# The last group of a convolution feed-forward layer written out, its down units run together, and the last stores cut smaller

## The chip, the cores and the metric

One core of a Trainium2 chip runs the kernel. The metric is device time in microseconds (us), the median of several runs. The kernel before took 2371.83 us (three runs, 2370.70 to 2373.25).

## What is computed

One decoder layer for 512 prompt tokens and 8 sample tokens, 2048 channels wide, everything in f32:

```python
h = RMSNorm(x); z = h @ w_in                      # mixers A, B, C from slices of z
x += concat(A, B, C) @ w_out
z = RMSNorm(x) @ w_up                             # 2048 -> 2 x 5632
zc = conv_b + sum(zp[:, j:j+T] * conv_w[j] for j in range(3))   # causal, depthwise, width 3
g, a = split(zc);  x += (silu(g) * a) @ w_down    # 5632 -> 2048
# outputs, among others: x (y_prompt, y_sample) and the last two rows of z before the convolution
# (ffn_conv_prompt; for the samples the new row, ffn_conv_sample)
```

The change touches only the feed-forward part and the outputs named in the last comment.

## The kernel before, in words

Tokens lie along the free dimension: `xT` holds 16 channel tiles of 128 partitions by 520 tokens (512 + 8). A matmul has a 128x128 weight block as stationary operand and half of the tokens, 260, as moving operand. For accuracy each f32 weight block is split into a rounded part and a rest, `whi` and `wlo`, and so are the activations, and three products are added: hi*hi, hi*lo, lo*hi. The work is cut into **units** of 1 MB of weights, each of four **quarters**; a quarter is 3 products x 4 blocks x 2 halves = 24 matmuls. For each quarter ACT copies raw weights to `whi` (`q_hi`, L812), POOL subtracts to get `wlo` (L1633), and TensorE (PE) runs the matmuls. `whi` and `wlo` are rings of four quarters, so ACT may convert a quarter when PE has done the quarter four before it (semaphore `w_used`); `raw` holds two units, filled by SyncE (SP) with `load_pair` (L1659) when POOL has split the unit two before.

The 44 tiles of the hidden layer go in 11 **groups** of four (`GC` = 4, `NG` = 11). A group has 8 **up units** (for each of its four tiles one for g and one for a, `up_mm`, matmuls at L415) and 4 **down units** (`down_mm`, L709), in which each quarter makes one of the 16 output tiles. For tile j the vector engine (DVE) reads the two up results (`read`, L1525, and the last 10 columns into `ztail`, L1528), ACT and DVE do the convolution (`conv`, L1538 and L1540), ACT the SiLU, DVE the gate `gm` (L1553), ACT `g_hi` (L1092), DVE `g_lo` (L1558). DVE also adds each down quarter into `xT` (semaphore `d_add`); quarters alternate between two PSUM bank pairs, so down quarter n waits for the addition of n-2.

The order is written out by hand for each engine, with semaphores between. Group 0 does its 8 ups. In the loop over groups 1 to 10, the order of one pass is: two ups of this group, the four down units of the **previous** group, the other six ups. So a group's gates are ready long before its downs, except in the last: behind the loop stand only the downs of group 10, which need the gate of the last tile (`g_lo` >= `NG*GC`), made from the last up unit.

Behind the loop PE also does three kinds of transposes. `turn_tail` (L769) turns four `ztail` tiles of 10 columns at a time, 22 times in all: six before the last downs, one behind each of the last down quarters but the first, and one at the very end; ACT reads each result to `trow` (L1124). `turn_y(dt)` (L778) turns output tile dt to token-major, one quarter behind the additions, and DVE reads it to `ytok` (L1147). At the end, when all tails are read, 16 transposes (L799) turn the sample tokens, and one ACT copy reads them (L1143). SP stores `y_prompt` in four pieces of four tiles (1 MB); before the fourth it waits for all tails and stores `trow` as two transfers, one of 2 partitions and one of 8, each partition 11264 floats long. The sample store is last, and SP waits for every store before it ends (L1751).

Of the kernel before, what the change touches and what calls it, by code (L numbers as in the profile page):

```python
# [21 lines left out]
F32 = mybir.dt.float32  # L22
# [5 lines left out]
P = 128  # L28
D = 2048
# [29 lines left out]
U_GRP = 2 * GC  # L59
U_ALL = U_FFN + NG * (U_GRP + GC)  # L60


# [18 lines left out]
def hybrid_layer(nc, io):  # L81
# [217 lines left out]
    par_rows = Region(fA.at, 2 * GC * P * 4).take("par_rows", [20, 2, GC * P])  # L299
    ytok = fA.take("ytok", [P, NB, D])  # L300
    fZ = r_z.again()
    trow = fZ.take("trow", [S + 2, F2])
    ytok8 = fZ.take("ytok8", [S, D])

    sems = {}
# [95 lines left out]
    def _(pe):  # L401
# [297 lines left out]

        def down_mm(q0, d0):  # L700

            for k in range(4):
                pe.wait_ge(w_lo, q0 + (k + 1))
                pe.wait_ge(s("d_add"), d0 + (k + 1))
                b = 4 + 2 * (k % 2)
                for kind, (w, x) in enumerate(((whi, g_hi), (whi, g_lo), (wlo, g_hi))):
# [55 lines left out]

        def turn_tail(r):

            b = 2 + r % 2
            if r >= 2:
                pe.wait_ge(s("t_read"), r - 1)
            for c in range(4):
                t = nc.tensor.transpose(ps[0:S + 2, b, c * P:(c + 1) * P], ztail[:, 4 * r + c, :], ident[:])  # L769
            t.then_inc(s("t_turn"), 1)  # L770

        def turn_y(dt):

            pe.wait_ge(s("d_add"), (NG - 1) * 16 + dt + 3)
# [6 lines left out]
        pe.wait_ge(z_free, U_FFN + 8 * NG + 2)  # L781
        tails = iter(range(FC // 2))
        for _ in range(6):
            turn_tail(next(tails))
        pe.wait_ge(s("g_lo"), NG * GC)
        for m in range(GC):
            for k in down_mm(4 * (U_ALL - GC + m), (NG - 1) * 16 + 4 * m):
                if 4 * m + k >= 1:
                    turn_y(4 * m + k - 1)
                    turn_tail(next(tails))  # L790
        turn_y(15)
        turn_tail(next(tails))
        assert next(tails, None) is None
        pe.wait_ge(s("t_read"), FC // 2)
        for q in range(4):
            if q == 0:
                pe.wait_ge(s("d_add"), NG * 16 + 2)
            for c in range(4):
                t = nc.tensor.transpose(ps[0:S, 4 + q, c * P:(c + 1) * P], xT[:, 4 * q + c, T:N], ident[:])  # L799
        t.then_inc(s("y8_turn"), 1)  # L800


    @block.scalar
    def _(act):
# [285 lines left out]
        def gated_hi(n, j):  # L1090
            act.wait_ge(s("f_m"), n + 1)
            nc.scalar.activation(g_hi[:, j, :], gm[:], ACT.Copy).then_inc(s("g_hi"), 1)  # L1092

        def ffn_group_act(q1, pair0, n0, grp, with_down):


            nonlocal n_group
            n_group = grp
            units = GC * 3 if with_down else U_GRP
            due = {} if with_down else {(1, 3): [(norm_root, 0)]}  # L1100
            for j in range(GC):
# [6 lines left out]
                due.setdefault(hi_at, []).append((gated_hi, j))  # L1108
            for u in range(1, units + 1):
                for k in range(4):  # L1110
                    q_hi(q1 + (4 * (u - 1) + k), k, u % 2, pair0 + 16 * (u // 2))
                    for step, j in due.get((u, k), []):
# [4 lines left out]
        n_group = 0  # L1117
        ffn_group_act(4 * U_FFN + 4, 8 * U_FFN + 16, 0, 0, False)
        with act.Fori(1, NG) as i:
            ffn_group_act(i * 48 + 4 * (U_FFN + U_GRP - 12 + 1), i * 96 + 8 * (U_FFN + U_GRP - 12 + 2), i * GC, i, True)  # L1120

        def read_tail(r):
            act.wait_ge(s("t_turn"), r + 1)
            nc.scalar.activation(trow[:, 512 * r:512 * r + 512], ps[0:S + 2, 2 + r % 2, :], ACT.Copy).then_inc(s("t_read"), 1)  # L1124

        r = 0
        for u in range(U_ALL - GC, U_ALL):
            for k in range(4):
                if u > U_ALL - GC:
                    q_hi(4 * u + k, k, u % 2, 16 * (u // 2 + 1))  # L1130
                    reads = 1
                else:
                    reads = 2
                for _ in range(reads):
                    if r < 6 or u > U_ALL - GC:
                        if r < FC // 2:
                            read_tail(r)
                            r += 1
        while r < FC // 2:
            read_tail(r)  # L1140
            r += 1
        act.wait_ge(s("y8_turn"), 1)
        nc.scalar.activation(ytok8[:], ps[0:S, 4:8, :].rearrange("p a n -> p (a n)"), ACT.Copy).then_inc(s("y8_read"), 1)  # L1143

# [7 lines left out]
    def _(dve):  # L1152
# [358 lines left out]

        def ffn_group_dve(u0, n0, d0, base, tail, with_down):

# [42 lines left out]
            def lo(n, j):  # L1556
                dve.wait_ge(s("g_hi"), n + 1)
                tt(g_lo[:, j, :], gm[:], g_hi[:, j, :].bitcast(F32), sub).then_inc(s("g_lo"), 1)  # L1558

            def down(m, k):  # L1560
                e = 4 * m + k
                dve.wait_ge(w_used, u0 * 4 + (4 * (2 + m) + k + 5))
                x2 = halves(xT[:, e, :])
                tt(x2, pair(4 + 2 * (k % 2)), x2, add).then_inc(s("d_add"), 1)  # L1564

            for j in range(GC):
                g = 2 * j + (GC if with_down and j else 0)
                n = n0 + j
                read(n, 0, g, j)
                read(n, 1, g + 1, j)  # L1570
                conv(n, 0, j)
                if with_down and j == 0:
                    down(0, 0)
                conv(n, 1, j)
                if with_down and j == 0:
                    down(0, 1)
                gate(n, j)
                if with_down and j == 0:
                    for e in range(2, 16):
                        down(e // 4, e % 4)  # L1580
                lo(n, j)
            return told[0]

        steps = ffn_group_dve(U_FFN, 0, None, 0, lambda half, j: FC * half + j, False)
        with dve.Fori(1, NG) as i:
# [60 lines left out]
    def _(sp):  # L1646
# [65 lines left out]
        def load_group(grp, col, split, with_down):  # L1712
# [4 lines left out]
            if not with_down:  # L1717
                load_pair(up(0), split)
                sp.wait_ge(w_used, USED_OUT)
            else:  # L1720
# [10 lines left out]
        load_group(0, 0, 4 * U_FFN - 4, False)  # L1731
        with sp.Fori(1, NG) as i:
            load_group(i, i * (GC * P), i * 48 + 4 * (U_FFN + U_GRP - 12) - 4, True)
        for m in (0, 2):
            load_pair([down_of((NG - 1) * GC * P, mm) for mm in (m, m + 1)],
                      4 * (U_ALL - GC + m) - 4, True)

        for q in range(4):
            if q == 3:
                sp.wait_ge(s("t_read"), FC // 2)  # L1740
                store(sp, io["ffn_conv_prompt"][0, 0], trow[0:2, :])
                store(sp, io["ffn_conv_sample"][0, :, 1, :], trow[2:2 + S, :])
            sp.wait_ge(s("y_read"), 4 * q + 4)
            store(sp, io["y_prompt"][0, :, q * 512:(q + 1) * 512].rearrange("(j p) d -> p j d", p=P),
                  ytok[:, :, q * 512:(q + 1) * 512])
        sp.wait_ge(s("y8_read"), 1)
        store(sp, io["y_sample"].rearrange("b t d -> (b t) d"), ytok8[:])
# [33 lines left out]
```

## Time and profile before

| | |
|---|---|
| median of three runs | 2371.83 us |
| profiled execution, its own time | 2365.21 us |
| its span in the profile | 2363.5 us |
| PE busy / weight loads | 2274.4 us (96%) / 2203.7 us |
| DVE, ACT, POOL busy | 863.3, 729.8, 940.3 us |
| mean granted clock of PE | 0.977 |
| DMA | 213.32 MB, 90 GB/s over the span |

The profiled execution's time is 1.7 us above its span and 6.6 us below the median of the runs. The page gives busy time by engine, then 40 slices with the busy share in tenths, the chain of waits that ended last, and the costliest groups of instructions. PE is busy nearly all the time; its slices are at 9 except around the attention stage and at the end, where the last slice shows 7.

### The profile page before, as it was taken

How to read it: one execution, taken by the hardware profiler on the slowest of the kernel's cores; microseconds unless marked ns; L12 is line 12 of the kernel's file. 1: busy time of each engine (PE TensorE's matmuls, PEld its weight loads, DVE VectorE, ACT ScalarE, POOL GpSimd, SP SyncE). 2: the span in 40 equal slices, each digit the busy share in tenths (PEclk: the TensorE clock that was granted, in tenths of full speed). 3: DMA queues.
4: the chain of work that ended last, by engine and by line, in shares of the span. 5: the costliest groups of instructions: out<-in, count | busy, mean ns of one | idle time of the engine just before them, and what ended most of it. 6: DMA issues, size and time to landing. Idle time of an engine off the chain costs nothing.

```text
span 2363.5 us, 45545 instructions
## 1 busy us (share of the span) xinstructions
PE 2274.4 (96%) x18446; PEld 2203.7 (93%) x18446; DVE 863.3 (37%) x1465; ACT 729.8 (31%) x1259; POOL 940.3 (40%) x735
## 2 busy tenths in 40 slices
PE   7999999876799999999999999999999999999997
PEld 7999887764799999999999999999999999999987
DVE  6112234477522243242433334243433324333332
ACT  4222232135433332232323223232322323233232
POOL 4443333200344444444444444444444444444431
PEclk9999999879999999999999999999999999999999
DMA  5532233510333232322223232222323333232323
GB/s 163 169 89 72 70 76 84 64 36 23 126 89 93 87 107 92 91 89 89 90 89 94 93 98 91 89 90 89 90 89 93 96 96 90 89 90 89 89 72 98
DMA packets 322074, 213.32 MB, mean 90 GB/s; under 512 B 11798, under 2 KB 296063, under 8 KB 321215
## 3 DMA queue, kind: packets, MB, share of 16 engines
q1 hardware_dynamic: 311971, 208.71, 29.0%
q10 hardware_dynamic: 10046, 3.80, 1.6%
q8 instruction: 42, 0.69, 0.1%
q14 instruction: 15, 0.12, 0.0%
HBM read 201.36 MB, written 11.49 MB: 90 GB/s over the span
## 4 chain that ended last, share of the span: by engine, by line
PE 88%; issue 5%; DVE 3%; POOL 2%; ACTq 1%; ACT 1%; DMA 0%; DVEq 0%; SPq 0%; POOLq 0%
PE ps L415 59%; PE ps L709 21%; POOL wlo L1633 2%; DVE nvar L393 1%; PE ps L667 1%; PE ps L380 1%; DVE sx L1433 0%; PE ps L645 0%; PE ps L769 0%; PE ps L657 0%; PE ps L499 0%; PE ps L508 0%; PE ps L507 0%; ACTq L935 0%; PE ps L553 0%
## 5 line engine op out<-in xcount | busy, mean ns | idle before, releaser
L1633 POOL TENSOR_TENSOR wlo<-raw,whi 128x512 fp32r<-128x512 f32 x712 | 932.4, 1312 | 1382.9 <-ACT whi L812 1259.3
L812 ACT ACTIVATE whi<-raw 128x512 fp32r<-128x512 f32 x712 | 447.9, 632 | 1326.7 <-PE ps L415 970.3
L415 PE MATMUL ps<-h_hi,whi 128*128 128x260 f32 x2816 | 395.1, 282 | 0.0
L415 PE MATMUL ps<-h_lo,whi 128*128 128x260 f32 x2816 | 393.5, 282 | 0.0
L415 PE MATMUL ps<-h_hi,wlo 128*128 128x260 f32 x2816 | 393.3, 282 | 0.0
L415 PEld LDWEIGHTS ps<-h_hi,wlo 128*128 128x128 f32 x2816 | 360.9, 188 | 0.0
L415 PEld LDWEIGHTS ps<-h_lo,whi 128*128 128x128 f32 x2816 | 360.6, 188 | 0.0
L415 PEld LDWEIGHTS ps<-h_hi,whi 128*128 128x128 f32 x2816 | 359.7, 188 | 0.4
L415 PE MATMUL ps<-act_hi,whi 128*128 128x260 f32 x1504 | 219.6, 289 | 13.3 <-DVE act_lo L1473 8.0
L415 PEld LDWEIGHTS ps<-act_hi,whi 128*128 128x128 f32 x1504 | 197.5, 193 | 21.1 <-issue 19.6
L1564 DVE TENSOR_TENSOR xT<-ps,xT 128x520 f32<-128x520 f32 x160 | 111.9, 700 | 287.8 <-PE ps L709 286.6
L415 PE MATMUL ps<-act_lo,whi 128*128 128x260 f32 x1504 | 214.2, 285 | 0.0
L415 PE MATMUL ps<-act_hi,wlo 128*128 128x260 f32 x1504 | 211.7, 283 | 0.0
L709 PE MATMUL ps<-g_lo,whi 128*128 128x260 f32 x1408 | 199.4, 284 | 0.0
L709 PE MATMUL ps<-g_hi,whi 128*128 128x260 f32 x1408 | 199.3, 284 | 0.0
L415 PEld LDWEIGHTS ps<-act_lo,whi 128*128 128x128 f32 x1504 | 196.8, 192 | 0.0
L709 PE MATMUL ps<-g_hi,wlo 128*128 128x260 f32 x1408 | 196.6, 282 | 0.0
L415 PEld LDWEIGHTS ps<-act_hi,wlo 128*128 128x128 f32 x1504 | 194.5, 190 | 0.0
L1525 DVE TENSOR_TENSOR za<-ps,rs 128x520 f32<-128x520 f32 x44 | 30.8, 700 | 418.8 <-PE ps L415 418.8
L709 PEld LDWEIGHTS ps<-g_lo,whi 128*128 128x128 f32 x1408 | 183.5, 189 | 0.0
L709 PEld LDWEIGHTS ps<-g_hi,whi 128*128 128x128 f32 x1408 | 180.4, 189 | 0.4
L709 PEld LDWEIGHTS ps<-g_hi,wlo 128*128 128x128 f32 x1408 | 180.0, 188 | 0.0
(296 smaller groups left out, 1444.8 us busy)
## 6 DMA issues: line engine op xcount, KB each, us to landing
raw<-in_w_up SPq DMA_DIRECT2D x88, 1024.0 KB, 5.2
raw<-in_w_down SPq DMA_DIRECT2D x44, 1024.0 KB, 5.0
raw<-in_w_in SPq DMA_DIRECT2D x30, 1024.0 KB, 5.0
raw<-in_w_out SPq DMA_DIRECT2D x16, 1024.0 KB, 5.5
x_spill<-xT SPq DMA_DIRECT2D x1, 4160.0 KB, 16.4
xT<-x_spill SPq DMA_DIRECT2D x1, 4160.0 KB, 12.5
xtok<-in_x_prompt SPq DMA_DIRECT2D x4, 1024.0 KB, 8.9
out_y_prompt<-ytok SPq DMA_DIRECT2D x4, 1024.0 KB
```

The lines of the kernel that those rows point to most:

```text
L380: mm = nc.tensor.matmul(ps[:, 6 + k % 2, :], pairones[:], nsq[:, k % 2, :], start=True, stop=True)
L393: link(nc.vector.reciprocal(nvar[:, k % 2, :], nvar[:, k % 2, :]))
L415: mm = nc.tensor.matmul(ps[:, bank + h, 0:NH], w[:, k, c, :], x[:, 4 * c + k, h * NH:(h + 1) * NH], start=(k == 0 and kind == 0 and c == 0 ...
L667: mm = nc.tensor.matmul(ps[64 * r:64 * r + 64, 7 * (n % 2), 0:P], vtb[:, i - 1 + kb, 64 * kv:64 * kv + 64], pt[:, n % 2, (2 * r + kb) * P: ...
L709: mm = nc.tensor.matmul(ps[:, b + h, 0:NH], w[:, k, c, :], x[:, c, h * NH:(h + 1) * NH], start=(kind == 0 and c == 0), stop=(kind == 2 and ...
L812: nc.scalar.activation(whi[:, k, :, :], rawq(k, slot), ACT.Copy)\
L1525: tt(halves(z[:, 2:]), pair(bank), halves(rs2[:]), mult).then_inc(s(name), 1)
L1564: tt(x2, pair(4 + 2 * (k % 2)), x2, add).then_inc(s("d_add"), 1)
L1633: nc.gpsimd.tensor_tensor(wlo[:, k, :, :], rawq(k, u), whi[:, k, :, :].bitcast(F32), ALU.subtract).then_inc(w_lo, 1)
```

## The change

The loop runs over groups 1 to 9. Group 10 is written out on every engine: its eight up units first, then the four down units of group 9, then its own four. Since both groups' gated values are alive together, group 10 has its own buffers `e_hi`, `e_lo` in the place of `ytok`, and `ytok` moves to the region of the normed input. On DVE and ACT the ups of group 10 follow the pattern of group 0; the 16 additions of group 9's downs are interleaved with the gate of its last tile.

The 88 tail tiles are turned 11 at a time (11 x 10 = 110 columns), 8 transposes in one place, between the second and third down unit of group 9; ACT reads them in two copies. The sample transposes are done four at a time behind `turn_y` of tiles 3, 7, 11 and 15, each read by its own ACT copy. The tails are stored as ten transfers, one for each row, ahead of the y stores, and the fourth y store becomes three: tiles 12 and 13, tile 14, tile 15.

```diff
-        with pe.Fori(1, NG) as i:
+        with pe.Fori(1, NG - 1) as i:
...
-        def turn_tail(r):
-            b = 2 + r % 2
-            if r >= 2:
-                pe.wait_ge(s("t_read"), r - 1)
-            for c in range(4):
-                t = nc.tensor.transpose(ps[0:S + 2, b, c * P:(c + 1) * P], ztail[:, 4 * r + c, :], ident[:])
+        def turn_tail():
+            pe.wait_ge(z_free, U_FFN + 8 * NG + 2)
+            for r in range(2 * FC // TT):
+                tails = ztail[:, TT * r:TT * r + TT, :].rearrange("p t s -> p (t s)")
+                t = nc.tensor.transpose(ps[0:TROWS, 2 + r // 4, (r % 4) * P:(r % 4 + 1) * P], tails, ident[:])
             t.then_inc(s("t_turn"), 1)
...
+            if dt % 4 == 3:
+                q = dt // 4
+                pe.wait_ge(s("t_read"), 2)
+                if q >= 2:
+                    pe.wait_ge(s("y8_read"), q - 1)
+                for c in range(4):
+                    t = nc.tensor.transpose(ps[0:S, 2 + q % 2, c * P:(c + 1) * P], xT[:, 4 * q + c, T:N], ident[:])
+                t.then_inc(s("y8_turn"), 1)
+        last = NG - 1
+        q0, use0 = 4 * U_LAST, last * 8 + U_FFN
+        up_units(q0, use0, 0, None, (last, last * 16 - 16))
+        for j in range(1, GC):
+            up_units(q0 + 8 * j, use0, j)
+        pe.wait_ge(s("par_ready"), last + 1)
+        pe.wait_ge(s("g_lo"), last * GC)
+        for m in range(GC):
+            for _ in down_mm(q0 + 4 * (U_GRP + m), last * 16 + 4 * m - 16):
+                pass
+            if m == 1:
+                turn_tail()
         pe.wait_ge(s("g_lo"), NG * GC)
         for m in range(GC):
-            for k in down_mm(4 * (U_ALL - GC + m), (NG - 1) * 16 + 4 * m):
+            for k in down_mm(q0 + 4 * (U_GRP + GC + m), last * 16 + 4 * m, e_hi, e_lo):
                 if 4 * m + k >= 1:
                     turn_y(4 * m + k - 1)
-                    turn_tail(next(tails))
         turn_y(15)
...
+        ffn_group_act(4 * U_LAST + 4, 8 * U_LAST + 16, (NG - 1) * GC, NG - 1, False, True)
+        for q in range(4):
+            act.wait_ge(s("y8_turn"), q + 1)
+            nc.scalar.activation(ytok8[:, 512 * q:512 * q + 512], ps[0:S, 2 + q % 2, :], ACT.Copy).then_inc(s("y8_read"), 1)
...
+        ffn_group_dve(U_LAST, (NG - 1) * GC, (NG - 2) * 16, (NG - 1) * steps,
+                      lambda half, j: (NG - 1) * GC + (FC * half + j), False, True)
...
+        sp.wait_ge(s("t_read"), 2)
+        for row in range(S + 2):
+            dst = io["ffn_conv_prompt"][0, 0, row] if row < 2 else io["ffn_conv_sample"][0, row - 2, 1]
+            store(sp, dst.rearrange("(r t n) -> t r n", t=TT, n=P), trow[row:TROWS:S + 2, :, :])
+        for first, tiles in ((0, 4), (4, 4), (8, 4), (12, 2), (14, 1), (15, 1)):
+            sp.wait_ge(s("y_read"), first + tiles)
+            cols = slice(first * P, (first + tiles) * P)
+            store(sp, io["y_prompt"][0, :, cols].rearrange("(j p) d -> p j d", p=P), ytok[:, :, cols])
+        sp.wait_ge(s("y8_read"), 4)
```

How the instructions stand. On PE before, behind the last up unit of group 10 (the loops' branches) come the tails and at once the group's own downs, whose first matmul waits for the last gate (`g_lo`):

```order
L415 MATMUL ps<-h_hi,wlo 128x260 x8
...
L748 COMPARE_AND_BRANCH
L769 MATMUL ps<-ident,ztail 10x128 [waits z_free]
L769 MATMUL ps<-ident,ztail 10x128 x7
L769 MATMUL ps<-ident,ztail 10x128 [waits t_read]
...
L709 MATMUL ps<-g_hi,whi 128x260 [waits d_add,w_lo,g_lo]
L709 MATMUL ps<-g_hi,whi 128x260 x7
L709 MATMUL ps<-g_lo,whi 128x260 x8
```

On PE now, the end of group 9's second down unit, the tails, the later start of group 10's own downs, and the first transposes between them:

```order
L714 MATMUL ps<-g_hi,wlo 128x260 x8
L773 MATMUL ps<-ident,ztail 110x128 [waits z_free]
L773 MATMUL ps<-ident,ztail 110x128 x7
L714 MATMUL ps<-g_hi,whi 128x260 [waits d_add,w_lo]
...
L714 MATMUL ps<-e_hi,whi 128x260 [waits d_add,w_lo,g_lo]
L714 MATMUL ps<-e_hi,whi 128x260 x7
L714 MATMUL ps<-e_lo,whi 128x260 x8
L714 MATMUL ps<-e_hi,wlo 128x260 x8
...
L782 MATMUL ps<-ident,xT 128x128 [waits d_add]
```

Sixteen down quarters now stand between the last up unit and the matmul that waits for the last gate, and the tails are no longer behind each quarter.

On DVE now, the last tile of group 10 with the first additions (L1567) of group 9's downs among its convolution; before, no addition stood there:

```order
L1542 SCALAR_TENSOR_TENSOR cg<-zg,cpar,cg 128x512
L1567 TENSOR_TENSOR xT<-ps,xT 128x520
L1540 SCALAR_TENSOR_TENSOR ca<-cpar,ca 128x8
L1542 SCALAR_TENSOR_TENSOR ca<-za,cpar,ca 128x512
L1567 TENSOR_TENSOR xT<-ps,xT 128x520
L1555 TENSOR_TENSOR gm<-cg,ca 128x520
L1561 TENSOR_TENSOR e_lo<-gm,e_hi 128x520
L1567 TENSOR_TENSOR xT<-ps,xT 128x520 x14
```

The third addition stands behind the gate and `e_lo`.

On SP, the stores at the end, before:

```order
L339 DMA out_y_prompt<-ytok 128x4x512 [waits y_read] x3
L339 DMA out_ffn_conv_prompt<-trow 2x11264 [waits t_read]
L339 DMA out_ffn_conv_sample<-trow 8x11264
L339 DMA out_y_prompt<-ytok 128x4x512 [waits y_read]
L339 DMA out_y_sample<-ytok_148 8x2048 [waits y8_read]
```

and now:

```order
L344 DMA out_ffn_conv_prompt<-trow 11x8x128 [waits t_read]
L344 DMA out_ffn_conv_prompt<-trow 11x8x128
L344 DMA out_ffn_conv_sample<-trow 11x8x128 x8
L344 DMA out_y_prompt<-ytok 128x4x512 [waits y_read] x3
L344 DMA out_y_prompt<-ytok 128x4x256 [waits y_read]
L344 DMA out_y_prompt<-ytok 128x4x128 [waits y_read] x2
L344 DMA out_y_sample<-ytok_149 8x2048 [waits y8_read]
```

The tails' stores moved ahead of every y store, and the last y store has 128 columns.

## Rows read from the trace of the kernel before

**Rows 1.** The page: span, and PE's busy time.
```profile
span 2363.5 us, 45545 instructions
PE 2274.4 (96%) x18446; PEld 2203.7 (93%) x18446; DVE 863.3 (37%) x1465; ACT 729.8 (31%) x1259; POOL 940.3 (40%) x735
```

**Rows 2.** Windows: stretch, length, busy of PE, PEld, DVE, ACT, POOL, PEclk, DMA, GB/s.
```profile
2220.00:2240.00 20.00, 20.00 (x170) 20.00 (x169) 8.79 (x13) 6.39 (x10) 9.11 (x7) 1.00 0.35 105
...
2280.00:2300.00 20.00, 16.25 (x115) 13.80 (x113) 7.47 (x14) 6.66 (x12) 2.58 (x2) 0.75 0.17 54
```

**Rows 3.** Chain of waits, last ups to the end: start us, us, what.
```profile
2239.96 37.51 PE ps L415 x314
...
2277.49 0.71 DVE za L1525
...
2284.87 3.58 PE ps L769 x16
2288.44 6.55 PE ps L709 x48
...
2295.43 0.44 PE ps L769 x4
2295.87 2.89 PE ps L709 x24
...
2347.66 0.44 PE ps L778 x4
...
2350.23 1.93 PE ps L799 x16
...
2352.18 1.87 ACT ytok L1143
```

**Rows 4.** Windows of 2 us around the wait for the last gate.
```profile
2278.00:2280.00 2.00, 0.45 (x4) 0.37 (x5) 1.74 (x4) 0.94 (x2) 1.27 (x1) 0.97 0.00 0
...
2288.00:2290.00 2.00, 2.00 (x12) 1.97 (x10) 0.00 (x0) 0.80 (x2) 0.00 (x0) 0.50 0.00 0
2290.00:2292.00 2.00, 2.00 (x18) 2.00 (x18) 0.00 (x0) 0.00 (x0) 0.00 (x0) 0.97 0.00 0
```

**Rows 5.** Timeline of DVE, one tile's gate inside the loop.
```profile
2093.02 0.70 DVE L1525 TENSOR_TENSOR za<-ps,rs 128x520 f32<-128x520 f32 x1 [9.43 <-PE ps L415]
...
2100.03 1.29 DVE L1553 TENSOR_TENSOR gm<-cg,ca 128x520 f32<-128x520 f32 x1 [0.50 <-ACT cg L1088]
2102.89 1.30 DVE L1558 TENSOR_TENSOR g_lo<-gm,g_hi 128x520 fp32r<-128x520 f32 x1 [1.57 <-ACT g_hi L1092]
```

**Rows 6.** Timeline of ACT, the same tile.
```profile
2102.17 0.62 ACT L1092 ACTIVATE g_hi<-gm 128x520 fp32r<-128x520 f32 x1
```

**Rows 7.** Timeline of the last 30 us, all engines.
```profile
2337.74 0.37 SPq L339 DMA_DIRECT2D out_y_prompt<-ytok  x1
...
2347.70 0.70 DVE L1591 TENSOR_TENSOR xT<-ps,xT 128x520 f32<-128x520 f32 x1 [2.46 <-PE ps L709]
...
2349.15 0.69 DVE L1147 COPY ytok<-ps 128x512 f32<-128x512 f32 x1 [0.15 <-PE ps L778]
2349.59 0.59 ACT L1124 ACTIVATE trow<-ps 10x512 f32<-10x512 f32 x1 [0.43 <-PE ps L769]
...
2350.86 1.17 SPq L339 DMA_DIRECT2D out_y_prompt<-ytok  x1
...
2354.07 2.88 SPq L339 DMA_DIRECT2D out_y_sample<-ytok  x1
```

**Rows 8.** Waits of SP's queue.
```profile
SPq L1751 <- DMA out_y_sample<-ytok: 6.0, 1, 6.0
```

**Rows 9.** Windows over the third y store, and over the end.
```profile
2340.00:2341.00 1.00, 1.00 (x12) 0.92 (x11) 0.82 (x2) 0.00 (x0) 0.00 (x0) 1.00 1.07 416
2341.00:2342.00 1.00, 1.00 (x11) 1.00 (x10) 0.48 (x1) 0.59 (x1) 0.00 (x0) 1.00 0.23 88
```

**Rows 10.** The same columns, half microseconds in the end.
```profile
2356.50:2357.00 0.50, 0.00 (x0) 0.00 (x0) 0.00 (x0) 0.00 (x0) 0.00 (x0) 0.50 0.14 53
```

**Rows 11.** DMA issues: engine, count, KB each, median us from issue to landing.
```profile
bst<-bias_rows SPq DMA_DIRECT2D x32, 64.0 KB, 1.9
```

More of the change, by code:

```diff
@@ L60 @@
 U_ALL = U_FFN + NG * (U_GRP + GC)
+U_LAST = U_ALL - U_GRP - 2 * GC
 def bucket_of(dist):
@@ L299, in hybrid_layer @@
     par_rows = Region(fA.at, 2 * GC * P * 4).take("par_rows", [20, 2, GC * P])
-    ytok = fA.take("ytok", [P, NB, D])
+    e_hi = fA.take("e_hi", [P, GC, N], F32R)
+    e_lo = fA.take("e_lo", [P, GC, N], F32R)
     fZ = r_z.again()
-    trow = fZ.take("trow", [S + 2, F2])
+    ytok = fZ.take("ytok", [P, NB, D])
     ytok8 = fZ.take("ytok8", [S, D])
+    TT = 11
+    TROWS = (S + 2) * TT
+    trow = fZ.take("trow", [TROWS, 2 * FC // TT, P])
     sems = {}
@@ L698, in up_mm, with down_mm @@
                 tile_mm(k, bank, whi, wlo, h2_hi, h2_lo)
-        def down_mm(q0, d0):
+        def down_mm(q0, d0, x_hi=g_hi, x_lo=g_lo):
             for k in range(4):
@@ L705, in down_mm @@
                 b = 4 + 2 * (k % 2)
-                for kind, (w, x) in enumerate(((whi, g_hi), (whi, g_lo), (wlo, g_hi))):
+                for kind, (w, x) in enumerate(((whi, x_hi), (whi, x_lo), (wlo, x_hi))):
                     for c in range(4):
@@ L760, in _ @@
                 up_units(q0 + jj * 8 + 16, use0 + jj * 2, 0)
[L763 to L769 removed]
+        def turn_tail():
[3 more added lines that the diff above has]
+                t = nc.tensor.transpose(ps[0:TROWS, 2 + r // 4, (r % 4) * P:(r % 4 + 1) * P], tails, ident[:])
             t.then_inc(s("t_turn"), 1)
         def turn_y(dt):
[L774 removed]
+            pe.wait_ge(s("d_add"), NG * 16 - 16 + dt + 3)
             if dt >= 2:
@@ L1091, in gated_hi, with ffn_group_act @@
             act.wait_ge(s("f_m"), n + 1)
[L1092 to L1098, printed above, removed]
+            nc.scalar.activation((e_hi if final else g_hi)[:, j, :], gm[:], ACT.Copy).then_inc(s("g_hi"), 1)
+        def ffn_group_act(q1, pair0, n0, grp, with_down, ends=False):
+            nonlocal n_group, final
+            n_group, final = grp, ends
             units = GC * 3 if with_down else U_GRP
-            due = {} if with_down else {(1, 3): [(norm_root, 0)]}
+            if ends:
+                units = U_GRP + 2 * GC
+            due = {} if with_down or ends else {(1, 3): [(norm_root, 0)]}
             for j in range(GC):
@@ L1108, in ffn_group_act @@
                 due.setdefault(hi_at, []).append((gated_hi, j))
-            for u in range(1, units + 1):
+            for u in range(1, units + (0 if ends else 1)):
                 for k in range(4):
                     q_hi(q1 + (4 * (u - 1) + k), k, u % 2, pair0 + 16 * (u // 2))
+                    if ends and (u, k) == (U_GRP + 3, 0):
+                        read_tail()
                     for step, j in due.get((u, k), []):
@@ L1115, in ffn_group_act, with read_tail @@
                         step(n0 + j, j)
-        n_group = 0
+        n_group, final = 0, False
         ffn_group_act(4 * U_FFN + 4, 8 * U_FFN + 16, 0, 0, False)
-        with act.Fori(1, NG) as i:
+        with act.Fori(1, NG - 1) as i:
             ffn_group_act(i * 48 + 4 * (U_FFN + U_GRP - 12 + 1), i * 96 + 8 * (U_FFN + U_GRP - 12 + 2), i * GC, i, True)
[L1122 to L1143, printed above, removed]
+        def read_tail():
+            for h in range(2):
+                act.wait_ge(s("t_turn"), 1)
+                nc.scalar.activation(trow[:, 4 * h:4 * h + 4, :].rearrange("p r n -> p (r n)"), ps[0:TROWS, 2 + h, :],
+                                     ACT.Copy).then_inc(s("t_read"), 1)
+        ffn_group_act(4 * U_LAST + 4, 8 * U_LAST + 16, (NG - 1) * GC, NG - 1, False, True)
+        for q in range(4):
+            act.wait_ge(s("y8_turn"), q + 1)
+            nc.scalar.activation(ytok8[:, 512 * q:512 * q + 512], ps[0:S, 2 + q % 2, :], ACT.Copy).then_inc(s("y8_read"), 1)
     def read_y(dve, dt):
@@ L1509, in _, with ffn_group_dve @@
         link(nc.vector.reciprocal(rs2[:], rs2[:]))
-        def ffn_group_dve(u0, n0, d0, base, tail, with_down):
+        def ffn_group_dve(u0, n0, d0, base, tail, with_down, ends=False):
             told = [0]
@@ L1557, in lo @@
                 dve.wait_ge(s("g_hi"), n + 1)
-                tt(g_lo[:, j, :], gm[:], g_hi[:, j, :].bitcast(F32), sub).then_inc(s("g_lo"), 1)
+                lows, highs = (e_lo, e_hi) if ends else (g_lo, g_hi)
+                tt(lows[:, j, :], gm[:], highs[:, j, :].bitcast(F32), sub).then_inc(s("g_lo"), 1)
             def down(m, k):
                 e = 4 * m + k
-                dve.wait_ge(w_used, u0 * 4 + (4 * (2 + m) + k + 5))
+                dve.wait_ge(w_used, u0 * 4 + (4 * ((U_GRP if ends else 2) + m) + k + 5))
                 x2 = halves(xT[:, e, :])
@@ L1718, in load_group @@
                 load_pair(up(0), split)
+            if isinstance(grp, int) and grp == 0:
                 sp.wait_ge(w_used, USED_OUT)
@@ L1731, in _ @@
         load_group(0, 0, 4 * U_FFN - 4, False)
-        with sp.Fori(1, NG) as i:
+        with sp.Fori(1, NG - 1) as i:
             load_group(i, i * (GC * P), i * 48 + 4 * (U_FFN + U_GRP - 12) - 4, True)
[L1734 to L1746, printed above, removed]
+        load_group(NG - 1, (NG - 1) * GC * P, 4 * U_LAST - 4, False)
+        for grp in (NG - 2, NG - 1):
+            for m in (0, 2):
+                load_pair([down_of(grp * GC * P, mm) for mm in (m, m + 1)],
+                          4 * (U_LAST + U_GRP + GC * (grp - NG + 2) + m) - 4, True)
+        sp.wait_ge(s("t_read"), 2)
[7 more added lines that the diff above has]
+        sp.wait_ge(s("y8_read"), 4)
         store(sp, io["y_sample"].rearrange("b t d -> (b t) d"), ytok8[:])
```

27 lines of the change are left out of this document (9 added, 18 removed).

## The prediction

> **What bounds the kernel now.** I read the page first: TensorE is busy 2274.4 of 2363.5 us [rows 1], so over most of the kernel only fewer or cheaper matmuls would help, and this change removes no matmul of the projections. Next I read windows over the stretch that the change touches. Inside the loop PE is busy without a gap at full clock, and the 20 us behind 2280 have 16.25 us busy at a mean clock of 0.75 [rows 2]: there the end of the ups meets the last downs. Then the chain of waits shows what that stretch is made of [rows 3]. The ups end at 2277.47 (2239.96 + 37.51). From 2277.49 the chain leaves PE for the last tile's read, convolution and gate, and comes back to it at 2284.87 for tail transposes; the last downs stand from 2288.1 on. From there every quarter is 2.89 us of down matmuls with 0.44 us of y transposes and 0.44 us of tail transposes between two quarters, until the last quarter ends at 2347.66; call this T. Behind T the chain still has 15.84 us, to 2363.50. So two stretches are in question: 2277.47 to T, 70.19 us, and T to the end, 15.84 us.
>
> **Part 1, the order of the last units.** The same units are run before and after (8 ups, 4 downs of group 9, 4 downs of group 10); what changes is what stands between them. I count from the end of the ups, leaving out group 9's four down units, which stood ahead of that point before and stand behind it now. A loop quarter is 37.51 / 314 x 24 = 2.87 us.
> - Before: 70.19 us.
> - After: 16 quarters of 2.89 us = 46.24 us. That quarter is already straight-line code, and the loop's is 2.87, so I charge nothing for writing 48 quarters (8 ups and 4 downs) out; were the 0.02 us real it would be 1.0 us more.
> - `turn_y` for tiles 0 to 13 stands before the last quarter ends: 14 x 0.44 = 6.16 us, as before.
> - The sample transposes of tiles 3, 7 and 11: three times four, at the 0.44 us of four tail transposes, whose width of 10 is nearest [rows 3] = 1.32 us. They come out of the 1.93 us behind T.
> - The tails: 8 transposes, 110 columns wide. Four of 10 columns and four of 128 columns both take 0.44 us, so the width does not matter and 8 cost 0.88 us. Before, there were 24 ahead of the downs and one set of four behind 14 quarters ahead of T.
> - The last gate's wait of about 10.6 us (2277.47 to 2288.1) goes: 16 quarters of group 9 lie over it, 46 us of cover for a chain that ran to 2288.1 with tails in it. What is late next is at the start of that cover, and it is the one new wait that I price.
>
> The new wait: DVE's third addition stands behind `e_lo`, and down quarter 4 of group 9 needs it (two bank pairs). I place the loop's rows from the moment that the last up is read [rows 5, 6], t = 0 at 2093.02. There `g_hi` starts at 9.15 and `g_lo` runs from 9.87 to 11.17. Both are set by ACT's place in the weight order, and they don't move as long as `gm` is ready by 9.1. It ended at 8.30 in the loop; now two additions of 0.70 us stand ahead of it, but the first falls into a gap in which DVE waited for ACT, and the SiLU comes no earlier, so I get about 8.8. The third addition then ends at 11.17 + 0.05 + 0.70 = 11.92 us, and PE wants to start that quarter at 4 x 2.87 = 11.47. Price 0.45 us, say 0.5. Nothing else queues on PE meanwhile, and DVE has caught up one quarter later (its work is 0.70 us in each 2.87). Bounds: 0 (DVE's 1.30 us operation could take 0.70 when POOL is quiet) to 3 us, if `gm` misses its place by a quarter.
>
> After: 46.24 + 6.16 + 1.32 + 0.88 + 0.5 = 55.1 us. Gain 15.1 us. In it is the slow clock: at 2288 to 2290 PE ran at 0.50, its lower level of 1.2 GHz, behind a stretch in which it was mostly idle, and was back at 2.4 GHz after 2290 [rows 4]. With no idle stretch this cost of about 2 us isn't paid; if it came back behind the new wait the gain would be less by as much. Bounds of part 1: 12 to 16.
>
> Straight-line code could be feared for its fetching. The rows above show the written-out quarter within 0.02 us of the looped one. The Trainium skill's page "Runtime: NRT & Kernel Launch", section "Instruction fetch mechanics", says that fetching runs ahead sequentially and is mostly hidden, and that it is taken branches that can break it; by that rule writing out costs nothing or saves, and the trace agrees on the first half, since no row here shows a branch that cost anything in the loop.
>
> **Part 2, what stands behind T.** Before: the last addition starts at 2347.70, the last `ytok` copy ends at 2349.84, the last tail copy at 2350.18; only then come the 16 sample transposes (1.93 us), one copy of 1.87 us, and the sample store at 2354.07, which takes 2.88 us to issue and is waited for another 6.0 us [rows 3, 7, 8]. The last 1 MB of y is issued at 2350.86 behind two tail stores. While those are under way the DMA engines move 53 GB/s at a share of 0.14 of 16 engines [rows 10], against 416 GB/s in the third y store, which was issued at 2337.74 and done by about 2341.2, 3.5 us later [rows 7, 9]. So the end is long partly by the serial chain and mostly because long rows of few partitions hold few engines.
>
> After, by the same rows: the `ytok` copy of tile 15 ends at T + 2.18 (2349.84 - 2347.66), and its store is issued to T + 2.6. PE does the last four sample transposes right behind `turn_y(15)`, to T + 1.9; ACT's copy is a 512-column one (0.59 us), so T + 2.55, about when SP is free. The sample store starts at T + 2.6. How long it takes, no row shows for an unloaded queue. Below: 1.9 us, a 64 KB load [rows 11]. Above: 8.9 us, what it took before. The third y store, 16 times as large, needed 3.5 us. I take 2.9, between the two unloaded rows. The end of tile 15's store (256 KB, issued 0.4 us earlier) should fall at or before it. Closing: the wait ended at 2354.07 + 2.88 + 6.0 = 2362.95, so 0.55 us. Sum: T + 6.05 against T + 15.84, gain 9.8 us; bounds 3.8 (8.9 us) to 10.8.
>
> What the ten tail stores cost: they are issued in the 13 us of a late down unit at about 0.3 to 0.4 us each, some 4 us of SP's queue, when no weight load is left behind them. The first y store may wait for them, but 30 us stand behind it. ACT's and DVE's remaining edits lie beside PE's 3.3 us quarters: 0.63 us weight copy, 0.70 and 0.69 us on DVE.
>
> Which engines a store gets is where the skill says more than the rows. The rows show 53 GB/s at 0.14 x 16 = 2.2 engines busy [rows 10], and the store in flight had 2 rows. The skill's page "DMA: Bandwidth & Descriptors", section "Why a DMA increments its semaphore by 16 and not by 1", says that a transfer is shared over the largest number up to 16 that divides its slowest dimension: 2 engines for 2 rows, 8 for the sample store; the trace agrees for the first. By that rule the sample store has 8 KB on each of 8 engines and is nearly all latency, as I have it; if it went to one engine, at 416 / 16 = 26 GB/s, its 64 KB would take 2.5 us and the end would be T + 8.2.
>
> **The sum.** 15.1 + 9.8 = 24.9 us from the profiled execution's own 2365.21: 2340.3. That execution lies 6.62 us below the median of the runs shown, so the forecast for the median is 2371.83 - 24.9 = 2346.9 us, 1.05% faster.
>
> **Rivals.**
> 1. *The end stays long.* The smaller y stores and the sample store queue behind each other and the last still takes its 8.9 us. For it: the issue of 2.88 us shows a queue that pushes back, and the last three stores have short runs. Against it: the third y store went through at 416 GB/s, and the tail stores are now 30 us earlier. Gain 15.1 + 3.8 = 18.9: 2352.9 us.
> 2. *The wait moves to the start of group 9's downs.* `gm` misses its place at 9.15, ACT holds up the weight copies queued behind it, and PE idles some 3 us; the clock fell after about as long a gap before [rows 4], so some 2 us more. For it: the margin is 0.4 us. Against it: the loop does the same work with 0.85 us to spare. Loss 4.5 beyond the forecast: 2351.4 us.
> 3. *Slower: straight-line code starves PE.* 48 quarters that ran from a loop are now fetched anew. It breaks even at 24.9 / 48 = 0.52 us for each quarter, and it is slower by the 0.2% that can be told from no change (4.7 us) from 0.62 us, a fifth of a quarter; at 0.65 us it gives 2378 us. Against it: the quarters of the last downs were straight-line already, at 2.89 us. For it only that 12 units in a row are more than 4.
>
> **How the numbers follow.** The forecast 0.75, rival 1 0.12, rival 2 0.08, rival 3 0.02, and 0.03 for no difference by a cause that I don't see. The range takes the upper bounds of the gain (16 + 10.8 = 26.8, with 2 us for the medians' own spread: 2343) and both rivals on the faster side, with the lower bound of part 1 in rival 1's case (12 + 3.8 = 15.8: 2356). About 2 in 10 are left for the far sides. Faster by more than 0.2%: 0.95; within: 0.03; slower: 0.02.
>
> **What will show it.** In the changed profile: PE without a gap at the end of the ups, and full clock through the last 100 us; a wait of half a microsecond in front of group 9's fifth down quarter, released by DVE; 3.3 us between additions of the last downs where it was 3.76; 8 tail transposes in about 0.9 us; the end 6 us behind the last down quarter. Wrong it would be if PE shows idle time for weights or for instructions in the written-out part, if a gap of more than 2 us stands at the seam with a clock of 0.5, or if the last store is still under way 10 us behind T.

## The result, and the profile after

The changed kernel took 2346.46 us (median of four runs, 2345.23 to 2351.65) against 2371.85 us (four runs); recorded ratio 0.9904, 95% interval 0.9881 to 0.9926. The forecast was 2346.9. The two medians alone differ by 25.4 us (a quotient of 0.9893), the ratio gives 22.8 us and its interval 17.5 to 28.2. So the total is known to some 5 us only, and the terms of the sum have to be judged in the profiles.

The page of the changed kernel, as [rows 1]:

```profile
span 2344.7 us, 45172 instructions
PE 2272.1 (97%) x18366; PEld 2202.9 (94%) x18366; DVE 866.7 (37%) x1465; ACT 719.0 (31%) x1242; POOL 941.0 (40%) x735
```

The two spans differ by 18.8 us only, not by the 24.9 that I had summed. The rest lies where neither kernel differs. The same row of both, the first group of the up matmuls (count, ns, first and last start), before and then changed:

```profile
L415 PE MATMUL ps<-h_hi,whi x2816: 277/282/472, 797.8 to 2275.3; 128*128 128x260 f32 x188
```
```profile
L420 PE MATMUL ps<-h_hi,whi x2816: 277/282/472, 803.9 to 2235.3; 128*128 128x260 f32 x188
```

The feed-forward part began at 797.8 in the one profile and at 803.9 in the other. I call this start H and the end of the last down quarter T, and compare stretches: H to T is 1549.9 us before and 1534.7 after (2338.64 - 803.9), 15.1 less; T to the end is 15.84 and 6.06, 9.8 less. Together 24.9.

The chain of waits of the changed kernel from the last up unit on, as [rows 3]:

```profile
2209.99 27.47 PE ps L420 x230
2237.46 8.65 PE ps L714 x72
...
2246.77 0.54 ACT e_hi L1102
...
2247.41 1.29 DVE e_lo L1561
2248.70 0.62 DVE xT L1567
...
2249.45 11.74 PE ps L714 x96
2261.20 0.87 PE ps L773 x8
2262.07 28.77 PE ps L714 x240
2290.84 0.44 PE ps L782 x4
2291.27 2.88 PE ps L714 x24
...
2301.24 0.43 PE ps L790 x4
...
2335.74 2.90 PE ps L714 x24
...
2340.55 0.59 ACT ytok L1145
```

The ups end at 2237.46 and the downs begin at once. The chain leaves PE one time, for the last gate and the addition behind it, and comes back at 2249.45. The tails are one piece of 0.87 us. A quarter with its y transposes takes 2.88 + 0.44 = 3.32 us, where it was 3.76. The windows, as [rows 2]:

```profile
2236.00:2256.00 20.00, 19.53 (x163) 19.35 (x162) 11.79 (x18) 6.09 (x10) 8.37 (x7) 1.00 0.33 105
2256.00:2276.00 20.00, 20.00 (x170) 20.00 (x169) 4.38 (x7) 4.88 (x9) 9.02 (x7) 1.00 0.16 55
```

The granted clock is 1.00 (2.4 GHz) where it had been 0.75 on average. The 0.47 us that PE misses in the first window is the new wait. Its timeline (ACT, DVE and PE), against the loop's [rows 5, 6]:

```profile
2244.70 1.12 DVE L1555 TENSOR_TENSOR gm<-cg,ca 128x520 f32<-128x520 f32 x1
...
2246.68 0.62 ACT L1102 ACTIVATE e_hi<-gm 128x520 fp32r<-128x520 f32 x1
...
2247.41 1.29 DVE L1561 TENSOR_TENSOR e_lo<-gm,e_hi 128x520 fp32r<-128x520 f32 x1 [1.59 <-ACT e_hi L1102]
...
2249.45 1.20 PE L714 MATMUL ps<-g_hi,whi 128*128 128x260 f32 x8 [0.47 <-DVE xT L1567]
```

Counted from the last up's read (2237.50), `gm` ended at 8.32 us (the prediction had 8.8), 0.86 us ahead of `e_hi`, and the matmul that waited started at 11.95, where the third addition had been put at 11.92.

The end, all engines, as [rows 7], and SP's wait, as [rows 8]:

```profile
2299.95 2.10 SPq L344 DMA_DIRECT2D out_ffn_conv_prompt<-trow  x2
2302.10 6.88 SPq L344 DMA_DIRECT2D out_ffn_conv_sample<-trow  x8
...
2338.66 0.70 DVE L1600 TENSOR_TENSOR xT<-ps,xT 128x520 f32<-128x520 f32 x1 [2.03 <-PE ps L714]
...
2340.11 0.69 DVE L1149 COPY ytok<-ps 128x512 f32<-128x512 f32 x1 [0.15 <-PE ps L782]
2340.55 0.59 ACT L1145 ACTIVATE ytok<-ps 8x512 f32<-8x512 f32 x1 [10.82 <-PE ps L790]
2341.24 0.46 SPq L344 DMA_DIRECT2D out_y_sample<-ytok  x1
```
```profile
SPq L1763 <- DMA out_y_sample<-ytok: 2.5, 1, 2.5
```

The sample store starts at T + 2.6 and is waited for 2.96 us from its issue. The ten tail stores took SP 9.0 us and were issued by 2308.98, 29.7 us ahead of T.

### The profile page after: what moved, and what is told of

Read it like the earlier page. It is cut to its first block, busy times and chain, and to the rows that moved or that the text cites. A ratio compares the mean times of both kernels' runs of the same rounds, so it can differ in the third digit from the quotient of the medians.

```text
span 2344.7 us, 45172 instructions
## 1 busy us (share of the span) xinstructions
PE 2272.1 (97%) x18366; PEld 2202.9 (94%) x18366; DVE 866.7 (37%) x1465; ACT 719.0 (31%) x1242; POOL 941.0 (40%) x735
## 4 chain that ended last, share of the span: by engine, by line
PE 88%; issue 4%; DVE 4%; POOL 2%; ACTq 1%; ACT 0%; DMA 0%; DVEq 0%; POOLq 0%
PE ps L420 60%; PE ps L714 22%; POOL wlo L1642 2%; DVE nvar L398 1%; PE ps L672 1%; PE ps L385 1%; DVE sx L1435 0%; PE ps L662 0%; PE ps L650 0%; PE ps L504 0%; PE ps L513 0%; PE ps L512 0%; PE ps L540 0%; ACTq L945 0%; PE ps L558 0%
## 5 line engine op out<-in xcount | busy, mean ns | idle before, releaser
L1567 DVE TENSOR_TENSOR xT<-ps,xT 128x520 f32<-128x520 f32 x160 | 111.7, 699 | 286.6 <-PE ps L714 285.5
L714 PE MATMUL ps<-g_lo,whi 128*128 128x260 f32 x1280 | 181.2, 284 | 0.0
L714 PE MATMUL ps<-g_hi,whi 128*128 128x260 f32 x1280 | 179.4, 282 | 0.5 <-DVE xT L1567 0.5
L714 PE MATMUL ps<-g_hi,wlo 128*128 128x260 f32 x1280 | 178.7, 282 | 0.0
L714 PEld LDWEIGHTS ps<-g_lo,whi 128*128 128x128 f32 x1280 | 166.6, 189 | 0.0
L714 PEld LDWEIGHTS ps<-g_hi,whi 128*128 128x128 f32 x1280 | 163.3, 188 | 0.6 <-issue 0.6
L714 PEld LDWEIGHTS ps<-g_hi,wlo 128*128 128x128 f32 x1280 | 163.7, 188 | 0.0
```

## The experiments

H, T and the spans of all profiles (T is the end of the last quarter in the chain):

| kernel | H | T | H to T | T to end | median us | ratio (interval) |
|---|---|---|---|---|---|---|
| before | 797.8 | 2347.66 | 1549.9 | 15.84 | 2371.85 | |
| changed | 803.9 | 2338.64 | 1534.7 | 6.06 | 2346.46 | 0.9904 (0.9881, 0.9926) |
| control | 803.1 | 2337.87 | 1534.8 | 6.03 | 2345.66 | 0.9895 (0.9872, 0.9919) |
| tails_only | 804.4 | 2346.28 | 1541.9 | 8.22 | 2355.79 | 0.9944 (0.9925, 0.9964) |
| samples_late | 804.3 | 2337.78 | 1533.5 | 7.92 | 2347.45 | 0.9908 (0.9887, 0.9930) |
| lo_later | 800.3 | 2334.36 | 1534.1 | 6.04 | 2341.94 | 0.9885 (0.9863, 0.9907) |
| one_last_store | 798.5 | 2333.28 | 1534.8 | 7.82 | 2344.31 | 0.9898 (0.9866, 0.9929) |
| samples_first | 800.7 | 2335.49 | 1534.8 | 6.21 | 2343.96 | 0.9891 (0.9859, 0.9923) |
| no_tail_stores | 804.0 | 2353.04 | 1549.0 | 9.26 | 2361.56 | 0.9974 (0.9964, 0.9984) |
| rows_split16 | 790.9 | 2339.97 | 1549.1 | 27.53 | 2379.94 | 1.0059 (1.0037, 1.0081) |
| rows_spread16 | 798.1 | 2347.11 | 1549.0 | 20.09 | 2369.88 | 1.0018 (1.0001, 1.0035) |

The first four after the changed kernel shared eleven runs of before with a median of 2369.69 us, the next four thirteen with 2366.87, the last one thirteen with 2368.16. So medians of different lines are not to be compared to the microsecond; ratios and stretches are.

### control: the changed kernel again

> The changed kernel once more, to measure it beside the kernel before on one chip and to see how the stage ahead of the feed-forward part varies. Theory (the change acts only behind the last up unit of group 9, and the 6 us that the two profiles differ ahead of it are the spread of the attention stage): ratio about 0.9895, some 25 us; the first h_hi matmul may stand anywhere between 797 and 805 us in either kernel, and T to the end stays 6.1 us. Rival (the longer program slows the earlier stage): the first h_hi matmul is always some 6 us later than in a profile of the kernel before, and the gain in a pair of runs with equal early stages stays near 19 us.

The stretches repeat to 0.1 us, and the ratio is the one expected. Its interval (19 to 30 us) is too wide to tell 24.9 from the rival's 19 with any margin; H is what speaks against the rival. H varies in every kernel: 790.9 to 804.0 in the four profiles with the old order of the last group and the old tails, 798.5 to 804.3 in the six of the changed one and its variants. With it goes the clock granted ahead of it: over the first 780 us it was 0.95 in rows_split16 (the earliest H), 0.94 in before, and 0.92 or 0.93 in all with H at 800 or later. A window of the attention stage in rows_split16 and in samples_late (among the latest):

```profile
400.00:620.00 220.00, 162.74 (x1190) 133.00 (x1189) 146.80 (x432) 87.48 (x235) 33.15 (x25) 0.85 0.30 63
```
```profile
400.00:620.00 220.00, 164.81 (x1103) 131.12 (x1103) 142.42 (x420) 86.51 (x234) 27.90 (x21) 0.77 0.26 53
```

With a clock of 0.85 more of the stage's matmuls fit into the window (1190 against 1103). So 6 us lie within the spread of that stage; the rival, that H is always some 6 us later with the longer program, falls by 798.5 in one_last_store and 804.0 in no_tail_stores. A smaller shift is not excluded: the mean H is 797.7 in the four profiles and 801.9 in the six.

### tails_only: the new tails in the old order

```diff
+            for r in range(2 * FC // TT):
+                tails = ztail[:, TT * r:TT * r + TT, :].rearrange("p t s -> p (t s)")
+                t = nc.tensor.transpose(ps[0:TROWS, 2 + r // 4, ...], tails, ident[:])
...
-        for _ in range(6):
-            turn_tail(next(tails))
+        turn_tail()
...
-                    turn_tail(next(tails))
```

> The kernel before with the tails alone changed: 8 transposes of 110 columns in the place of the first six turns, two copies, ten stores ahead of the y stores. Group order, sample transposes and the four y stores are as before. Theory: 14 x 0.44 = 6.2 us go between the last quarters, the downs start at about 2285.2 instead of 2288.1 on the clock of the profile before (2.9 us), and the end shortens from T + 15.8 to about T + 8.9: 16 us in all, 2355.8 by the median before. Rival (the order of the group brings most): at most 10 us, and the end stays above T + 12 because y and the samples are still late.

H to T fell by 8.0 us, not 9.1, and the end to T + 8.22 (expected 8.9); 15.6 us of the 24.9. The missing microsecond is in the wait that stayed. PE's timeline around it:

```profile
2286.17 1.93 PE L769 MATMUL ps<-ident,ztail 128*110 128x128 f32 x8 [2.09 <-DVE ztail L1510]
2291.82 2.10 PE L711 MATMUL ps<-g_hi,whi 128*128 128x260 f32 x8 [3.72 <-DVE g_lo L1540]
2293.72 1.94 PE L711 MATMUL ps<-g_lo,whi 128*128 128x260 f32 x8
2295.45 1.58 PE L711 MATMUL ps<-g_hi,wlo 128*128 128x260 f32 x8
2296.86 1.12 PE L711 MATMUL ps<-g_hi,whi 128*128 128x260 f32 x8
```

and a window in it:

```profile
2292.00:2293.00 1.00, 1.00 (x5) 1.00 (x6) 0.00 (x0) 0.00 (x0) 0.00 (x0) 0.50 0.00 0
```

The downs start 7.7 us after the last up matmul instead of 10.6, as expected. But most of the first quarter ran at 1.2 GHz: from 2291.82 to 2296.86 is 5.04 us for what takes 2.87, 2.2 us lost. Before, the first two quarters took 6.9 us (2288.1 to 2294.99, [rows 3]) for 5.8, 1.1 us lost; but there 16 tail transposes stood directly in front of them, from 2284.87 on, at the low clock too:

```profile
2284.87:2288.10 3.23, 3.23 (x17) 1.68 (x17) 0.27 (x1) 2.07 (x4) 0.00 (x0) 0.50 0.02 5
```

They took 3.2 us, where 16 at full clock take 4 x 0.44 = 1.8. So before lost 1.1 us in the downs and, by this estimate, another 1.5 in the transposes. With the transposes gone the downs themselves met the low clock, and their additional loss of 1.1 us is what was missing. The rival (at most 10 us, end above T + 12) is out.

### samples_late: the sample transposes at the end again

```diff
-            if dt % 4 == 3:
-                q = dt // 4
...
+        for q in range(4):
+            for c in range(4):
+                t = nc.tensor.transpose(ps[0:S, 4 + q, c * P:(c + 1) * P], xT[:, 4 * q + c, T:N], ident[:])
```

> The changed kernel with one part undone: all 16 sample transposes at the end, read by one copy. Theory (the serial chain behind T is lengthened by 1.5 us of transposes and 1.3 us of copy, while 1.3 us go from the stretch ahead of T): end at T + 8.9 instead of T + 6.1, net 1.5 us slower than the changed kernel. Rival (the end is set by the y store, not the samples): T + 6 to 7, net not slower.

T came 1.3 us earlier and the end at T + 7.92, 1.9 later than in the changed kernel, where I expected 2.8; net 0.6 us where I expected 1.5, which the medians don't resolve. The chain grew as expected (16 transposes in 1.76, one copy in 1.87 us), but the sample store, now issued 2.5 us later behind the y stores, was done 2.3 us after its issue instead of 2.96. This kernel and tails_only differ in the order of the group, with the buffers and the place of the tail transposes that go with it, and in the split of the last y store: the order is 1541.9 - 1533.5 = 8.4 us.

### lo_later: the new wait removed

```diff
-                if adds and ends:
-                    lo(n, j)
                 if adds:
                     for e in range(2, 16):
                         down(e // 4, e % 4)
+                        if ends and e == 3:
+                            lo(n, j)
```

> The changed kernel with e_lo of the last tile placed behind the fourth addition instead of in front of the third. Theory (PE's only wait in the written-out part is the third addition behind e_lo): PE's wait of 0.5 us at group 9's fifth down quarter disappears, T and the end are 0.5 us earlier, within the noise of the median. Rival (the wait is ACT's or the weights'): the gap stays where it is.

No wait of PE is left between the first and the last down. DVE's third addition no longer stands behind the gate, and `e_lo` took 0.69 us there, not 1.29:

```profile
2242.62 0.70 DVE L1567 TENSOR_TENSOR xT<-ps,xT 128x520 f32<-128x520 f32 x1 [0.39 <-PE ps L714]
...
2246.04 0.69 DVE L1561 TENSOR_TENSOR e_lo<-gm,e_hi 128x520 fp32r<-128x520 f32 x1
```

H to T is 0.7 us less than in the changed kernel, about the wait. It has the best ratio of all, 0.9885, but the intervals overlap; the gain over the changed kernel is shown in the trace alone.

### no_tail_stores: what the tail stores cost at the end

```diff
-                store(sp, io["ffn_conv_prompt"][0, 0], trow[0:2, :])
-                store(sp, io["ffn_conv_sample"][0, :, 1, :], trow[2:2 + S, :])
```

> The kernel before without the two stores of trow (ffn_conv_prompt and the new rows of ffn_conv_sample are not written). Theory (long rows of 2 and 8 partitions hold the DMA queue and make the end long): the y store takes 0.4 us to issue, the sample store starts at T + 6.4 as before, issues in 0.5 us and lands 2.5 us later: end T + 10, 5.9 us less than before. Rival (the serial chain and the 1 MB y store set the end): end above T + 14.

This kernel leaves two outputs unwritten. The end is T + 9.26, so these two stores of 440 KB cost 6.6 us at their old place; expected 5.9. The rival (above T + 14) is out. With them gone the last 1 MB of y moves at full rate while the samples are turned, a window of which is:

```profile
2358.00:2359.00 1.00, 0.00 (x0) 0.00 (x0) 0.00 (x0) 1.00 (x1) 0.00 (x0) 1.00 1.06 414
```

### rows_split16 and rows_spread16: why they are slow

```diff
+                for row in range(S + 2):
...
+                    store(sp, dst.rearrange("a (k n) -> a k n", k=16), trow[row:row + 1, :].rearrange("a (k n) -> a k n", k=16))
```

> The kernel before with the same rows stored at the same place, but as ten transfers, each one row cut in 16 pieces of 704 floats. Theory (it is the number of engines that a transfer is shared over, not its bytes): no stretch at 50 GB/s; the ten issues cost SP 0.35 to 0.9 us each, so the y store is issued at T + 6.5 to T + 11.5 and the end is at T + 11 to T + 16. Rival (bytes out of few partitions are slow whatever the number of engines): the slow stretch stays and the end is beyond T + 18.

The end moved to T + 27.5, beyond both. But the pieces of a row are contiguous and had been joined: the packet records show ten pieces of 45 KB. So it shows something else, ten long pieces. Windows while they run, and near the end:

```profile
2350.00:2351.00 1.00, 0.00 (x0) 0.00 (x0) 0.00 (x0) 0.00 (x0) 0.00 (x0) 0.50 0.10 45
...
2362.00:2363.00 1.00, 0.00 (x0) 0.00 (x0) 0.00 (x0) 0.00 (x0) 0.00 (x0) 0.50 0.11 45
...
2364.00:2365.00 1.00, 0.00 (x0) 0.00 (x0) 0.00 (x0) 0.00 (x0) 0.00 (x0) 0.50 0.06 25
```

The last piece starts at 2362.2, more than 10 us after the last transfer was issued at 2350.9. A piece stands in the window in which it starts, with all its bytes and time, so a window with long pieces gives no rate; the piece's own record does. They run one behind the other from 2343.24 to 2363.88, as on one engine: eight of them take 1.67 to 1.97 us (27 GB/s for most), two take 4.4 and 2.6 while y moves. Behind them 25 GB/s of y are left, a sixteenth of the 416 GB/s of all engines. So here the end is long because one engine has ten rows ahead of its share of y.

The same records correct a reading of the prediction. It took the 53 GB/s at a share of 0.14 [rows 10] for the 2-row store on 2.2 engines. The rows stand earlier, in the profile of before, with a share above 1 because each is counted whole at its start:

```profile
2351.00:2352.00 1.00, 1.00 (x11) 0.69 (x8) 0.00 (x0) 0.00 (x0) 0.00 (x0) 1.00 2.32 270
```

The bytes in [rows 10] are 2 KB pieces of y (26 of them between 2356 and 2357), while six of the ten long pieces were still under way. A long piece took 3.5 to 7.6 us there, though each lies in a partition of its own, against 1.7 us for one by itself. The second kernel keeps the pieces apart by leaving four floats of each out:

```diff
+                    store(sp, dst.rearrange("a (k n) -> a k n", k=16)[:, :, 0:700],
+                          trow[row:row + 1, :].rearrange("a (k n) -> a k n", k=16)[:, :, 0:700])
```

> The kernel before with its rows stored at the same place as ten transfers, each one row as 16 pieces of 700 floats (4 floats of every 704 are left out, so that the pieces can't be joined; in rows_split16 they were, and each row was one piece of 11264 floats on one engine). Theory (what is slow is a row that is one long piece on one engine): all 16 engines share each row, no engine is held, and the end falls from T + 27.5 in rows_split16 to about T + 14, which is T + 2.6 for the last tail, 8 us for issuing ten transfers and 3.5 us for the last. Rival (bytes out of one partition are slow whatever the number of engines): beyond T + 20.

```profile
2355.00:2356.00 1.00, 0.00 (x0) 0.00 (x0) 0.00 (x0) 0.00 (x0) 0.00 (x0) 1.00 1.15 34
...
2357.00:2358.00 1.00, 0.00 (x0) 0.00 (x0) 0.00 (x0) 0.00 (x0) 0.00 (x0) 0.50 1.34 87
...
2364.00:2365.00 1.00, 0.00 (x0) 0.00 (x0) 0.00 (x0) 0.00 (x0) 0.00 (x0) 0.50 1.18 399
```

Now the ten rows are shared over all 16 engines, and still move slowly: 20 to 87 GB/s in the windows from 2352 to 2361, where the same engines move 399 GB/s of y out of 128 partitions. The packet records say why: from 2352 to 2356 nearly every piece of 2.8 KB takes about 1.55 us, while thirty of the 160, later on, take 0.11, so the engines are not slow by themselves. Sixteen pieces in 1.55 us are 29 GB/s, hardly more than the one engine of rows_split16. Spreading took 7.4 us off the end (27.5 to 20.1), so the one engine was a part of it, as the theory says; but T + 14 was not reached, and the rival's T + 20 was: what one partition gives does not grow with the engines. Of the 6 us over the forecast, about 3 are SP's, which took 10.9 us to issue the ten rows and not 8, and about 3 stand behind that. What the rows show of the changed kernel's form, 11 partitions in pieces of 512 bytes, is 0.9 us of SP for each of ten transfers, and 0.03 us for a piece, at a place where nothing waits for them. Whether that form would also have been cheap at the old place was not tried.

### one_last_store and samples_first: the end's fine cut

```diff
-        for first, tiles in ((0, 4), (4, 4), (8, 4), (12, 2), (14, 1), (15, 1)):
+        for first, tiles in ((0, 4), (4, 4), (8, 4), (12, 4)):
```

> The changed kernel with tiles 12 to 15 stored as one 1 MB transfer again. Theory (the 1 MB store, at over 400 GB/s, is done 3.5 us after its issue at T + 2.2, and the samples queue behind it): end T + 6.3 to 7.0, at most 0.9 us later than the changed kernel. Rival (the split is a main part of the gain at the end): 3 us or more later.

End T + 7.82, 1.8 us later than with three stores: between the theory (0.9 at most) and the rival (3). SP's wait:

```profile
SPq L1763 <- DMA out_y_sample<-ytok: 4.3, 1, 4.3
```

The sample store behind 1 MB was done 4.7 us after its issue, 1.8 later than behind 256 KB. So the split is worth 1.8 us where the sample store follows at once.

```diff
+            if first == 15:
+                sp.wait_ge(s("y8_read"), 4)
+                store(sp, io["y_sample"].rearrange("b t d -> (b t) d"), ytok8[:])
             sp.wait_ge(s("y_read"), first + tiles)
```

> The changed kernel with the sample transposes ahead of turn_y of tiles 3, 7, 11 and 15, and the sample store ahead of tile 15's. Theory (the last issued store ends last, whichever it is, since both are mostly latency): end T + 5.8 to 6.6, no difference that can be measured. Rival (256 KB in 512-byte pieces are slow): 1 us or more later.

End T + 6.21, as expected, and now the y store is last:

```profile
SPq L1764 <- DMA out_y_prompt<-ytok: 2.8, 1, 2.8
```

3.2 us from issue to the end of the wait for 256 KB, 2.96 for the samples' 64 KB: four times the bytes cost 0.2 us more, so both are mostly latency, as the theory said.

## Why the prediction was right

**The order and the last gate.** The sum for the stretch to T was 15.1 us, and H to T gave 15.1. The mechanism was as predicted: 16 quarters over the last gate's chain, and one new wait, by DVE's third addition. Its terms stood: 2.88 to 2.90 us for a quarter, 0.87 us for the tails (0.88), 0.43 to 0.44 us for four sample transposes, 0.47 us for the new wait (0.45, taken as 0.5), full clock. That the wait was the addition behind `e_lo` was shown by removing it. tails_only and samples_late split the stretch: 8.0 us by the tails, 8.4 us by the order, less 1.3 us for the three sets of sample transposes that now stand in it.

**The end.** T + 6.06 for 6.05. The sum took 2.9 us for the sample store, measured 2.96; that it hit this closely is luck, since 2.9 was a choice between 1.9 and 3.5, and the same store took 2.3 us in samples_late and 4.7 in one_last_store. Taken away one by one, the tail stores at the end are 6.6 us (no_tail_stores), the split of y 1.8 (one_last_store), the samples' turning between the quarters 1.9 (samples_late). These add to 10.3 and not to 9.8, since the parts overlap. In a row they close: the tails 7.6 (before to tails_only, 15.84 to 8.22; a last turn of tails behind T goes with the stores), then the split and the order 0.3 (to samples_late, 7.92), then the samples 1.9 (to 6.06). So the split is worth 0.3 us as long as the samples are late, and 1.8 once they are not.

**The offset.** Putting the sum on the median and not on the profiled execution's own time was right, for a reason that the prediction didn't have: that profile had an early H, 797.8, which goes with a time below the median, though no other execution of before has its H on record. Had I carried 2340.3 over, the forecast would have been 6 us low. That the median came within 0.5 us is luck: the interval of the ratio spans some 11 us.

**What was off.** The ten tail stores took SP 9.0 us, not some 4; each took 0.86 to 1.05 us to issue and not 0.3 to 0.4. Nothing waited for SP there. The slow clock of before, put at about 2 us, was 1.1 in the downs and an estimated 1.5 in the transposes ahead of them. The explanation of the slow end by the number of engines was half of it, and its row was misread: [rows 10] shows y behind the long rows, not the rows. rows_spread16 had all 16 engines at work and was still slow out of a single partition. None of this touches the sum, which had the sample store's time from other rows and the tail stores out of the way. The Trainium skill's page "DMA: Bandwidth & Descriptors", section "Why a DMA increments its semaphore by 16 and not by 1", says how many engines share a transfer: the largest number up to 16 that divides the slowest dimension on both of its sides. The trace agrees for rows_spread16 (16 pieces to a row, a share near 1) and for the sample store of before (8 rows, recorded as 8 pieces of 8 KB).

**The rivals.** 1 (the end stays long) is out: 2.96 us, not 8.9. 2 (the wait moves to the seam): it did move there, at a tenth of the rival's price (0.47 us against 5); `gm` had 0.86 us to spare. What that rival feared of the clock is real: in tails_only the gap in front of the downs cost another 2.2 us by the low clock behind it. 3 (straight-line code starves PE) is out: PE has no gap in the written-out quarters but the one, and none in lo_later. Nor did writing out save time: 2.88 to 2.90 us for a quarter against 2.87 in the loop.

## What to carry to other kernels

Where a loop is software-pipelined, ask what its last pass leaves without cover, and write that pass out so that independent work of the pass before lies over the last dependent chain. Small work put between the units of the engine that sets the time is not free: 14 of the 22 sets of four transposes cost 6.2 us, and with eleven narrow tiles packed into one stationary operand all 88 tiles took 0.9. At the end, count from the last matmul, and keep stores out of few partitions away from it. When two profiles are compared, compare the stretches that the change touches, since an unchanged stage can differ by more than the effect.

## What the runs showed of the hardware

A transpose with 10 columns of stationary operand takes as long as one with 110 or 128 (0.11 us each in a row at full clock). One SBUF partition gave about as much to 16 DMA engines (29 GB/s, 16 pieces of 2.8 KB in 1.55 us, rows_spread16) as to one (27 GB/s, 45 KB in 1.67 us, rows_split16), while all 16 move 399 to 416 GB/s out of 128 partitions. What a gap costs by the clock is not told by its length alone; it depends on what stands first behind it: in tails_only (gap of 7.7 us with 8 transposes in it) the downs met the clock of 0.50 and lost 2.2 us, in before (10.6 us, 24 transposes in it) the last 16 of these transposes met it first, and the downs lost 1.1.
